# Row sums of the FFN's down projection: from GpSimd subtractions to ScalarE negatives and accumulating transfers

## The reference

```python
def conv_ffn(x, w_up, w_ffn_conv, b_ffn_conv, w_down):
    hid = jnp.einsum('bsd,df->bsf', x, w_up)                  # 2048 -> 2 * 5632
    hid = causal_dwconv(hid, w_ffn_conv, b_ffn_conv)
    val, gate = hid[..., :D_FF], hid[..., D_FF:]
    return jnp.einsum('bsf,fd->bsd', jax.nn.silu(gate) * val, w_down)   # 5632 -> 2048
...
x = layer_norm(alpha * x + ff, ln2_g[l], ln2_b[l])
```

## Time and profile before

| | |
|---|---|
| time, median of 3 runs | 2170.28 us (2167.21 to 2173.6) |
| profiled execution, its own time | 2173.76 us |
| its span | 2171.9 us |
| mean granted PE clock | 0.993 |
| PE busy | 2117.2 us, 97% of the span |
| DVE busy | 1592.0 us, 73% |
| ACT busy | 949.6 us, 44% |
| POOL busy | 265.7 us, 12% |

### The profile page before, as it was taken

The page is one execution under the profiler, slowest core; times in us unless marked ns, Lnnn a source line. Parts: engine busy times, 40 slices in busy tenths (PEclk is TensorE's granted clock), DMA queues, the critical chain, the costliest instruction groups (busy, mean ns, idle before and its releaser), DMA issues. The chain is left out here.

```text
span 2171.9 us, 26843 instructions
## 1 busy us (share of the span) xinstructions
PE 2117.2 (97%) x10583; PEld 1793.4 (83%) x10583; DVE 1592.0 (73%) x1860; ACT 949.6 (44%) x1107; POOL 265.7 (12%) x241
## 2 busy tenths in 40 slices
PE   9999999999999998999999999999999999999995
PEld 7888888888888887788888888888888787888874
DVE  4354424423338997988888888888888788999998
ACT  4332222221123446555555555555555554444442
POOL 0000000000001304011111111111111023221220
PEclk9999999999999999999999999999999999999998
DMA  6222222242227626898888887887777887775463
GB/s 239 97 97 78 90 89 93 78 166 97 96 87 232 177 68 166 217 249 229 219 211 210 243 221 204 206 232 217 201 190 203 271 246 201 207 240 144 142 192 78
DMA packets 93754, 375.88 MB, mean 173 GB/s; under 512 B 8908, under 2 KB 21228, under 8 KB 80320
## 3 DMA queue, kind: packets, MB, share of 16 engines
q1 hardware_dynamic: 63328, 263.22, 34.3%
q0 software_dynamic: 30304, 110.99, 26.4%
HBM read 326.46 MB, written 26.21 MB: 162 GB/s over the span
## 5 line engine op out<-in xcount | busy, mean ns | idle before, releaser
L2062 PE MATMUL ps<-xb,slot_hi 128*128 128x512 f32 x2408 | 607.0, 394 | 11.7 <-DVE hid L1532 11.7
L2062 PEld LDWEIGHTS ps<-xb,slot_hi 128*128 128x128 f32 x2408 | 434.6, 190 | 91.9 <-issue 13.6
L2066 PEld LDWEIGHTS ps<-xb,slot_lo 128*128 128x128 f32 x2400 | 327.9, 191 | 23.6
L2066 PE MATMUL ps<-xb,slot_lo 128*128 128x256 f32 x2400 | 334.9, 282 | 0.0
L772 ACT ACTIVATE w_hi<-raw 128x2048 fp32r<-128x2048 f32 x56 | 107.4, 1918 | 424.4 <-PE ps L1783 421.9
L1154 DVE TENSOR_TENSOR w_lo<-raw,w_hi 128x2048 fp32r<-128x2048 f32 x55 | 125.9, 2289 | 213.7 <-ACT w_hi L772 213.7
L1781 PE MATMUL ps<-act_hi,w_hi 128*128 128x512 f32 x640 | 249.7, 390 | 0.0
L1783 PE MATMUL ps<-act_hi,w_lo 128*128 128x512 f32 x640 | 249.1, 389 | 0.0
L1782 PE MATMUL ps<-act_lo,w_hi 128*128 128x512 f32 x640 | 249.0, 389 | 0.0
L1501 DVE TENSOR_TENSOR slot_lo<-unit_odd,slot_hi 128x1024 fp32r<-128x1024 f32 x153 | 187.5, 1225 | 37.6 <-ACT slot_hi L974 37.4
L974 ACT ACTIVATE slot_hi<-unit_odd 128x1024 fp32r<-128x1024 f32 x154 | 163.1, 1060 | 108.6 <-PE ps L2066 75.6
(11 more groups left out here) (238 smaller groups left out, 3431.8 us busy)
## 6 DMA issues: line engine op xcount, KB each, us to landing
raw<-w_mix SPq DMA_DIRECT2D x56, 1024.0 KB, 4.9
unit_odd<-w_up SPq DMA_DIRECT2D x88, 512.0 KB, 6.5
unit_even<-w_up SPq DMA_DIRECT2D x84, 512.0 KB, 6.5
da<-w_down SPq DMA_DIRECT2D x16, 2048.0 KB, 12.6
unit_odd<-w_up POOLq DMA_DIRECT2D x44, 512.0 KB, 8.5
unit_even<-w_up POOLq DMA_DIRECT2D x42, 512.0 KB, 8.6
da<-w_down POOLq DMA_DIRECT2D x20, 1024.0 KB, 9.7
oa<-w_out SPq DMA_DIRECT2D x6, 2048.0 KB, 7.9
```

Of the source, the lines that this page charges most:

```text
L2062: pe.matmul(bank, hi[:, P * j:P * j + P], xb[:, i, j, :, :].rearrange("p r t -> p (r t)"), start=fresh and j == 0, stop=False, skip_group_ ...
L2066: last = pe.matmul(bank[:, 256:512], lo[:, P * j:P * j + P], xb[:, i, j, 0, :], start=False, stop=j == 7, skip_group_check=not fresh)
```

## The change

The four subtractions T1 to T4 are taken from POOL in every chunk (in chunk 0 T1 and T2 stay on DVE). In their place ACT writes a negative and POOL issues a transfer that adds a block of `h_dram` to it: T1 is `hy` = -H11, plus H12; T2 is `hb11` = -T1, plus H22; T3 is `hb12` = -H12, plus H22; T4 is `hy` = -T2, plus H21. ACT makes the negatives in the third slot of a product: T3's in P1, T4's in P6, T1's and T2's of the next chunk in P3 and P4. T2's negative has to wait on ACT until T1's transfer has landed. In POOL's order T1 and T2 of the next chunk stand after S1 and, in chunk 0, after the residual transfers. T3 goes between the two S3. SP waits for T4's negative instead of T4, and loads `hb21` directly after `hb11`, no longer after P4's remainder. The counters of S2 and S4 are merged into one semaphore each (`s2_sum`, `s4_sum`), with offsets; nothing else is done with them.

```diff
             for c in range(CHUNKS - 1):
-                sp.wait_ge(t4_sum, OUT_CHUNKS + c + 1)
+                sp.wait_ge(h_neg, negations(c, 4))
                 load_hidden(c + 1, 0, hb11)
+                load_hidden(c + 1, 2, hb21)
                 sp.wait_ge(down_lo, slot_no(c, 4, 0))
                 load_block(c + 1, A21, da21)
...
-                sp.wait_ge(hc_lo, NP * c + 7)
-                load_hidden(c + 1, 2, hb21)
                 sp.wait_ge(down_lo, SLOT0[c + 1])
                 load_block(c + 1, A22, da22)
...
-            def down_t1(c, g):
-                for b in range(2):
-                    pool.wait_ge(hb_in[b], 16 * (c + 1))
-                pool.wait_ge(hc_lo, NP * c)
-                pool.tensor_tensor(hy[:, 0:g, :], hb12[:, 0:g, :], hb11[:, 0:g, :], ALU.subtract).then_inc(t1_sum, 1)
...
+            def add_hidden(c, b, dst, done):
+
+                g = CHUNK_PAIRS[c]
+                t = 2 * sum(CHUNK_PAIRS[:c]) + (g if b >= 2 else 0)
+                pool.dma_start(dst[:, 0:g, :],
+                               h_dram[t:t + g, :, 256 * (b % 2):256 * (b % 2) + 256].rearrange("k p t -> p k t"),
+                               accum_op=ALU.add).then_inc(done, 16)
+
+            def down_t1(c):
+                pool.wait_ge(h_neg, negations(c, 1))
+                add_hidden(c, 1, hy, t124_in)
...
+            for i in range(2):
+                pool.wait_ge(h_out[i], 16 * (NF // 2))
             for c in range(CHUNKS):
                 g = CHUNK_PAIRS[c]
-                if c:
-                    down_t1(c, g)
-                    down_t2(c, g)
                 for p in range(0, g, 2):
                     down_s3(c, p)
-                down_t3(c, g)
+                    if p == 0:
+                        down_t3(c)
                 if c == 1:
                     add_residual(0, 1, NP)
-                down_t4(c, g)
+                down_t4(c)
                 if c == 0:
                     add_residual(0, 0, 2)
                 if c + 1 < CHUNKS:
...
                 if c == 0:
                     add_residual(1, 1, 5)
                     add_residual(1, 0, 6)
+                if c + 1 < CHUNKS:
+                    down_t1(c + 1)
+                    down_t2(c + 1)
...
+            def negated(dst, src, c):
+                g = CHUNK_PAIRS[c]
+                act.activation(dst[:, 0:g, :], src[:, 0:g, :], ACT.Copy, scale=-1.0).then_inc(h_neg, 1)
+
+            def sum_starts(c, i, p):
+
+                if p != 2:
+                    return
+                at_p5 = NP * c + ORDER.index("P5") + 1
+                if i == 0:
+                    if c == 0:
+                        act.wait_ge(t1_sum, OUT_CHUNKS + 1)
+                    act.wait_ge(hb_in[1], 16 * (c + 1))
+                    negated(hb12, hb12, c)
+                elif i == 2:
+                    if c:
+                        act.wait_ge(t124_in, sums_in(c, 2))
+                    else:
+                        act.wait_ge(t2_sum, OUT_CHUNKS + 1)
+                    act.wait_ge(hc_lo, at_p5)
+                    negated(hy, hb11, c)
+                elif i == 5 and c + 1 < CHUNKS:
+                    act.wait_ge(hb_in[0], 16 * (c + 2))
+                    act.wait_ge(hc_lo, NP * (c + 1))
+                    negated(hy, hb11, c + 1)
+                elif i == 6 and c + 1 < CHUNKS:
+                    act.wait_ge(t124_in, sums_in(c + 1, 1))
+                    act.wait_ge(hc_lo, NP * (c + 1) + 1)
+                    negated(hb11, hy, c + 1)
...
                 if s + DOWN_AHEAD < N_DOWN:
                     down_split(s + DOWN_AHEAD)
+                sum_starts(c, i, p)
```

More of the change, by code:

```diff
@@ L26 @@
 NP = len(ORDER)
+LAST_S4_ON_DVE = 0
 N_UP = NP * GROUPS
@@ L54 @@
 OUT_S2 = {(5, 3): [0, 1], (6, 3): [2, 3]}
+S2_UP = OUT_CHUNKS * OUT_PAIRS
+S2_DOWN = S2_UP + GROUPS
+S4_LAST = OUT_CHUNKS * OUT_PAIRS
+S4_DOWN = S4_LAST + LAST_S4_ON_DVE
 FIN = [2, 3, 0, 1]
@@ L265, in build @@
         oa_in = [sem(f"oa_in{i}") for i in range(4)]
-        s2_out, s4_out = sem("s2_out"), sem("s4_out")
+        s2_sum, s4_sum = sem("s2_sum"), sem("s4_sum")
         tokens_hi, yc_lo = sem("tokens_hi"), sem("yc_lo")
@@ L279, in build @@
         s3_up = [sem(f"s3_up{i}") for i in range(2)]
-        s2_up, s4_up = sem("s2_up"), sem("s4_up")
+        s4_up = sem("s4_up")
         up_hi, up_lo, up_done = sem("up_hi"), sem("up_lo"), sem("up_done")
@@ L292, in build @@
         s3_added = [sem(f"s3_added{i}") for i in range(2)]
-        s2_down, s4_down = sem("s2_down"), sem("s4_down")
         t1_sum, t2_sum, t3_sum, t4_sum = sem("t1_sum"), sem("t2_sum"), sem("t3_sum"), sem("t4_sum")
         hc_lo = sem("hc_lo")
+        h_neg, t3_in, t124_in = sem("h_neg"), sem("t3_in"), sem("t124_in")
         down_hi, down_lo, down_done, half_done = sem("down_hi"), sem("down_lo"), sem("down_done"), sem("half_done")
@@ L374, in sums_after, with negations, sums_in @@
             return todo
+        def negations(c, t):
+            return 4 * c + {1: -1, 2: 0, 3: 1, 4: 2}[t]
+        def sums_in(c, t):
+            return 16 * (c + 1 if t == 3 else 3 * c + {1: -1, 2: 0, 4: 1}[t])
         def out_blocks(c):
@@ L457, in _ @@
             load_out(0, A22, oa22)
-            sp.wait_ge(s2_out, 4)
+            sp.wait_ge(s2_sum, 4)
             sp.wait_ge(out_lo, 4 * 2)
@@ L464, in _ @@
             sp.wait_ge(out_lo, 4 * 6)
-            sp.wait_ge(s4_out, 4)
+            sp.wait_ge(s4_sum, 4)
             load_out(1, A12, oa12)
@@ L621, in out_s3 @@
             def out_s3(c, p):
-                pool.wait_ge(s2_out, 4 * c + p + 2)
+                pool.wait_ge(s2_sum, 4 * c + p + 2)
                 pool.wait_ge(out_lo, 4 * NP * c + p + 2)
@@ L658, in up_s3 @@
                 pool.wait_ge(up_lo, NP * (m - 1) + 1)
-                pool.wait_ge(s2_up, m)
+                pool.wait_ge(s2_sum, S2_UP + m)
                 pool.dma_start(unit[m % 2][:, A11, :], w_up[2 * m + 1][:, 0:1024], accum_op=ALU.add
@@ L696, in down_s3 @@
                 n, w = sum(CHUNK_PAIRS[:c]) + p, min(2, CHUNK_PAIRS[c] - p)
-                pool.wait_ge(s2_down, n + w)
+                pool.wait_ge(s2_sum, S2_DOWN + n + w)
                 pool.wait_ge(down_lo, slot_no(c, 0, p) + w)
@@ L700, in down_s3, with down_t2, down_t3, down_t4 @@
                                accum_op=ALU.add, max_dma_last_dim=4096).then_inc(s3_added[p // 2], 16)
-            def down_t1(c, g):
-                for b in range(2):
-                    pool.wait_ge(hb_in[b], 16 * (c + 1))
-                pool.wait_ge(hc_lo, NP * c)
-                pool.tensor_tensor(hy[:, 0:g, :], hb12[:, 0:g, :], hb11[:, 0:g, :], ALU.subtract).then_inc(t1_sum, 1)
[L708 to L725, removed]
+            def add_hidden(c, b, dst, done):
[7 more added lines that the diff above has]
+                add_hidden(c, 1, hy, t124_in)
+            def down_t2(c):
+                pool.wait_ge(h_neg, negations(c, 2))
+                add_hidden(c, 3, hb11, t124_in)
+            def down_t3(c):
+                pool.wait_ge(h_neg, negations(c, 3))
+                add_hidden(c, 3, hb12, t3_in)
+            def down_t4(c):
+                pool.wait_ge(h_neg, negations(c, 4))
+                add_hidden(c, 2, hy, t124_in)
             for p in range(0, CHUNK_PAIRS[0], 2):
@@ L892, in out_split @@
                 else:
-                    act.wait_ge(s2_out if what == "P6" else s4_out, 4 * c + p + 1)
+                    act.wait_ge(s2_sum if what == "P6" else s4_sum, 4 * c + p + 1)
                 act.activation(oslot_hi[s % OUT_SLOTS][:, :], out_weights(what)[:, p, :], ACT.Copy).then_inc(out_hi, 1)
@@ L972, in up_split @@
                 else:
-                    act.wait_ge({"P6": s2_up, "P3": s4_up}[what], m if what == "P6" else 16 * m)
+                    act.wait_ge({"P6": s2_sum, "P3": s4_up}[what], S2_UP + m if what == "P6" else 16 * m)
                 act.activation(slot_hi[(n + 2) % 3][:, :], unit[m % 2][:, BLOCK[ORDER[i]], :], ACT.Copy).then_inc(up_hi, 1)
@@ L1081, in down_split @@
                 else:
-                    act.wait_ge({"P6": s2_down, "P3": s4_down}[what], n + 1)
+                    act.wait_ge({"P6": s2_sum, "P3": s4_sum}[what], {"P6": S2_DOWN, "P3": S4_DOWN}[what] + n + 1)
                 src = (da11, da12, da21, da22, dx)[BLOCK[what]]
@@ L1097, in hid_split @@
                     act.wait_ge(hb_in[{"P1": 0, "P2": 2, "P3": 3}[what]], 16 * (c + 1))
+                elif c == 0 and what in ("P6", "P5"):
+                    act.wait_ge({"P6": t2_sum, "P5": t1_sum}[what], OUT_CHUNKS + 1)
                 else:
-                    act.wait_ge({"P6": t2_sum, "P5": t1_sum, "P7": t3_sum, "P4": t4_sum}[what], OUT_CHUNKS + c + 1)
+                    act.wait_ge(t3_in if what == "P7" else t124_in, sums_in(c, {"P6": 2, "P5": 1, "P7": 3, "P4": 4}[what]))
                 src = {"P1": hb11, "P2": hb21, "P6": hb11, "P5": hy, "P7": hb12, "P3": hb22, "P4": hy}[what]
@@ L1384, in out_s2 @@
```

(14 more changed lines are left out.)

## The result

The changed kernel takes 2184.2 us (median of 5 runs, 2183.67 to 2186.37) where the kernel before takes 2170.28 (5 runs, 2167.21 to 2173.6): 13.9 us more, a ratio of 1.0064, 95% interval [1.0052, 1.0075]. The point of the forecast, 2176.2, is 8.0 us too low; the time lies inside the range, near its high end, and in the case "slower". The profiled execution took 2186.37 us, the slowest of the five.

What follows compares the result with a forecast made beforehand. PE was taken as the bound, with matmuls in flight for 97% of the span. Terms +5.4 (chunk 1), +1.7 (clock) and -1.2 (chunk 5) gave +5.9 on the median 2170.28: 2176.2 us, with an 8-in-10 range of 2168 to 2187.

Steps and rivals of the forecast that it cites:

- the case "slower": Outcome in which the changed kernel is slower by more than about 0.3%, 6.5 us; chance 0.45.
- T1 of chunk 1 and its price: Start of chunk 1: T1 lands at 1809.5, PE stands still 8.9 us, delay 9.8 us.
- In place of 4.4: Start of chunk 1: the 9.8 us delay replaces old waits of 2.70 and 1.74 us, net +5.4 us.
- Chunk 5, -1.2: P2 of chunk 5: a 0.8 us wait for T1 replaces 2.0 us removed; ends -2.0 and +3.1, +4.8 with clock.
- the nearest row: Accumulating transfer in the same load stream, issued at 2084.8, landed after 10.8 us; taken as chunk 5 T1's landing time.
- the first rival: Chunk 5: each T1 piece waits for one piece of other loads, PE stops 5 us; +11.9, 2182.2 us; chance 0.21.
- the 318 against 323: Pieces moved in 8 us, SP's 1 KB loads against POOL's 4 KB; cited as evidence for turns of one piece.
- The clock: After chunk 1's standstill PE runs a stretch at clock 0.50: +1.7 us, bounds 0 and twice that.
- The other chunks' T1 and T2 at nothing: Chunks 2 to 4: T1 has 14.9 us to land, T2 over 8 us; no cost, up to 2 us each.
- The negatives and the transfers as such at nothing: 22 negatives on ACT, at most 23 us, and 60 us of accumulating transfers are covered and cost PE nothing.
- the full queue: Rival: added transfers fill the DMA queue, S1, T1, T2 of chunks 2 and 3 late; about +12, 2182; chance 0.11.
- the starving: Rival: POOL's transfers starve beside busy DVE, +3.4 us in chunks 1 and 5 each; +12.7, 2183.0; chance 0.05.

Runs made afterwards that it cites:

- the second profile: The kernel before, with nothing edited, profiled a second time: 2169.49 us.
- the last run above: Changed kernel with chunk 1's T1 issued ahead of both residual transfers, T2 between them, LayerNorm's rows held until chunk 5's T2 landed: 2167.77 us, ratio 0.9986.

## Why the prediction was right and where it was wrong

The time lies in the range because the range was wide enough for a late T1 in chunk 5, not because the sum was right: two of its terms were too small by 4 and 6 us, and both errors point the same way.

*T1 of chunk 1 and its price: right.* The landing was put at 1809.5 and came at 1810.02, the standstill at 8.9 us and was 8.33 (place and releaser as described), and P2 of chunk 1 began at 1818.6, 11.0 us after 1796.7 + 10.9, where 9.8 and 1.7 for the clock were reckoned. Moving T1's issue took 9.5 us of it away (87.20 to 77.70), moving T2's too the rest.

*"In place of 4.4": wrong.* The sum set off the waits of 2.70 and 1.74 us as won, and then added the result to the median. Those waits were in the one profiled execution, which I knew to be 3.5 us above the median, and not in the second profile, whose time is the median's. Against that second profile chunk 1 lost 87.20 - 76.10 = 11.1 us; the term said 5.4 + 1.7 = 7.1.

*Chunk 5, -1.2: the term that was mis-sized most.* Chunks 4 and 5 together came out at +5.1 (-1.0 and 67.30 - 61.20). I took the landing after 10.8 us from the nearest row, an accumulating transfer of 4 KB pieces that hardly met the LayerNorm's rows. T1's landed after 15.4 us, close to the upper bound's 15.1. The two queues while each of them moved, first in the kernel before from 2088.9 to 2095.7, then in the changed kernel from 2089.4 to 2099.8:

```profile
q0 software_dynamic: 358, 1.40, 103.9%
q1 hardware_dynamic: 24, 0.07, 2.7%
```

```profile
q1 hardware_dynamic: 372, 2.95, 70.4%
q0 software_dynamic: 399, 0.39, 23.5%
```

That row had the engines nearly to itself; T1 had them for a quarter of the time. The mechanism is that of the first rival, turns of one piece; its 5.1 us of standstill were 5.95 and its time was 2182.2. I had its evidence, the 318 against 323, and gave it half the chance of the row that suited less. The Trainium skill (DMA: Bandwidth & Descriptors, SWDGE vs HWDGE vs iDMA) has packets, preferably of up to 4096 B, as the unit of a turn; the counts of 318 to 321 and 208 to 208 above do not agree with four 1 KB pieces in one.

*The clock: right in kind, too small.* It was expected once and came twice, 2.6 and 2.2 us in place of 1.7; together that is more than the bound of twice 1.7. What the prediction read off the trace before, that pauses of 2.7 us and less leave the clock at 1.00, held there but not in the last run above.

*The other chunks' T1 and T2 at nothing: right, and close.* T1 of chunks 2 and 3 landed 14.4 and 14.0 us after their issue; 14.9 were reckoned as free. ACT waited, PE did not. The 15.1 us that the sum started from were not the longest on this queue, as it says: the residual issued at 1781.29 in the kernel before took 16.9.

*The negatives and the transfers as such at nothing: right,* to within 1.5 us, by the last experiment. So the full queue and the starving were rightly small; chunks 2 and 3 of the changed kernel took 76.30 and 76.10 us. Of the starving rule (the Trainium skill, SBUF — State Buffer, SBUF: two separate sides) nothing was seen; the Trainium skill has it for DVE's two-port modes, and says that an operation on two tensors has none. T1 of chunk 5 landed after 10.0 us in place of 15.4 once the rows were gone, with DVE as busy as before, 55.78 against 55.54 us.

The account, against the second profile: 11.1 in chunk 1 and 5.1 in chunks 4 and 5 are 16.2 of the 16.9 us between the two executions' own times (2186.37 and 2169.49). By medians it is 13.9, since the changed kernel's profiled execution lies 2.2 us above its median and the second profile's 0.8 below that of the kernel before.

## What to carry to other kernels

Before a wait is booked as a gain, look whether it is in more than one execution: a profiled execution above the median can hold losses that most executions don't have. When an engine that feeds others has to wait for a transfer that it started itself, reckon the whole round trip (issue, what is ahead in that queue, turns with the other queue, landing, and every operation queued behind) and place the issue by that, since moving the wait alone moves the stall. A transfer of small pieces that is short of time should not share the engines with large pieces; hold those back, or cut them small.

## What the runs showed of the hardware

Two queues on the same DMA engines moved equal numbers of pieces whatever the sizes, which is what turns of one piece give: 318 pieces of mostly 8 and 12 KB against 321 of 1 KB in 8 us, 208 against 208 of mostly 1 KB in 2 us. DVE's subtractions of L1655 took up to 3.98 us beside POOL's, and at most 1.23 us where POOL's were cut to one column or taken away. One and the same load took 27.9 us in one execution of a kernel and 21.2 in another. PE's granted clock was 0.50 after standstills of 8.33 and 5.95 us, and after a pause of 2.52 us; after pauses of 2.36 and 2.70 us in other runs it was 1.00.
